# Feed-forward products with 512 moving columns, later start loads, and token parts of x made beside the router logits

## The reference

```python
def _hier_moe(x, w_grp, b_grp, w_exp, b_exp, w_gate, w_up, w_down):
    grp_logits = (xf @ w_grp + b_grp)                # 4 groups
    exp_logits = (xf @ w_exp + b_exp)                # 32 experts, 8 in a group
    # best group, two best experts in it, then for each chosen expert e:
    hdn = jax.nn.silu(xb @ w_gate[e]) * (xb @ w_up[e])
    y = hdn @ w_down[e]                              # weighted and added per token
# second block, four times, d_ff = 2816:
    y = (silu(x @ gate) * (x @ up)) @ down           # x <- norm(ALPHA * x + 0.5 * y)
```

## Time and profile before

| | us |
|---|---|
| median of 3 runs | 2418.55 |
| the 3 runs | 2409.77, 2421.46, 2418.55 |
| the profiled execution | 2419.57 |
| its span, first to last instruction | 2417.6 |
| PE busy | 2214.3 |
| DVE busy | 1076.5 |
| ACT busy | 734.3 |

### The profile page before, as it was taken

The page is one execution under the profiler, slowest core; times in us unless marked ns, Lnnn a source line. Parts: engine busy times, 40 slices in busy tenths (PEclk is TensorE's granted clock), DMA queues, the critical chain, the costliest instruction groups (busy, mean ns, idle before and its releaser), DMA issues.

```text
span 2417.6 us, 32311 instructions
## 1 busy us (share of the span) xinstructions
PE 2214.3 (92%) x13534; PEld 1641.1 (68%) x13534; DVE 1076.5 (45%) x1606; ACT 734.3 (30%) x1123; POOL 60.4 (2%) x62
## 2 busy tenths in 40 slices
PE   7978998799898889978988999988999999888998
PEld 7874443343377845424433899888998999788997
DVE  4663221121167722211212655666556555666555
ACT  3432110011134321101111444443444444543443
POOL 0010000000010100000000000001000000001000
PEclk9989999899997799999999999989999999979999
DMA  9437999999962389999999746523554565423551
GB/s 295 132 141 313 420 421 421 417 420 420 400 205 69 133 328 420 421 420 416 420 421 401 242 165 209 161 84 114 183 192 163 186 209 192 140 70 116 181 192 52
DMA packets 231548, 622.79 MB, mean 258 GB/s; under 512 B 15456, under 2 KB 166944, under 8 KB 182112
## 3 DMA queue, kind: packets, MB, share of 16 engines
q1 hardware_dynamic: 225952, 604.99, 66.1%
q0 software_dynamic: 3040, 10.78, 1.3%
q10 hardware_dynamic: 2400, 4.83, 0.6%
HBM read 619.51 MB, written 1.05 MB: 257 GB/s over the span
## 4 chain that ended last, share of the span: by engine, by line
PE 42%; DMA 6%; DVE 4%; ACT 1%; issue 1%; SPq 0%; POOL 0%; DVEq 0%; ACTq 0%
PE bank L228 28%; PE bank L1486 9%; PE bank L1326 3%; DMA wide_tables<-in_moe_w_up 1%; DMA x_tok<-in_moe_w_up 1%; DMA ring<-in_moe_w_up 1%; DMA w_parts<-in_moe_w_up 1%; DMA ring<-in_ffn_gate 1%; PE bank L1647 1%; DVE w_low L429 1%; DVE x_tok L674 0%; DVE x_tok L663 0%; DVE bn L652 0%; PE bank L469 0%; ACT w_high L422 0%
## 5 line engine op out<-in xcount | busy, mean ns | idle before, releaser
L429 DVE TENSOR_TENSOR w_low<-ring,w_high 128x1024 fp32r<-128x1024 f32 x364 | 440.6, 1225 | 374.2 <-ACT w_high L422 374.1
L228 PE MATMUL bank<-xT_high,w_high 128*128 128x256 f32 x1712 | 488.3, 285 | 20.4 <-DVE xT_low L491 12.0
L228 PE MATMUL bank<-xT_low,w_high 128*128 128x256 f32 x1712 | 486.5, 284 | 0.0
L228 PE MATMUL bank<-xT_high,w_low 128*128 128x256 f32 x1712 | 486.2, 284 | 0.0
L422 ACT ACTIVATE w_high<-ring 128x1024 fp32r<-128x1024 f32 x364 | 376.6, 1052 | 296.2 <-PE bank L228 274.6
L1326 PE MATMUL bank<-ring,arena 128*64 128x512 f32 x1344 | 339.4, 594 | 18.2 <-DMA ring<-in_moe_w_up 6.0
L228 PEld LDWEIGHTS bank<-xT_high,w_high 128*128 128x128 f32 x1712 | 330.2, 193 | 26.1 <-DVE xT_low L491 12.0
L228 PEld LDWEIGHTS bank<-xT_low,w_high 128*128 128x128 f32 x1712 | 330.4, 193 | 2.8
L228 PEld LDWEIGHTS bank<-xT_high,w_low 128*128 128x128 f32 x1712 | 330.3, 193 | 0.0
L1326 PE MATMUL bank<-w_parts,arena 128*64 128x512 f32 x768 | 259.1, 596 | 14.4 <-DMA w_parts<-in_moe_w_up 6.6
L1326 PEld LDWEIGHTS bank<-ring,arena 128*64 128x64 f32 x1344 | 111.2, 137 | 230.5 <-issue 221.6
(11 more groups left out here) (285 smaller groups left out, 2860.4 us busy)
## 6 DMA issues: line engine op xcount, KB each, us to landing
ring<-in_moe_w_gate SPq DMA_DIRECT2D x56, 1024.0 KB, 23.6
ring<-in_moe_w_up SPq DMA_DIRECT2D x56, 1024.0 KB, 22.7
ring<-in_moe_w_down SPq DMA_DIRECT2D x56, 1024.0 KB, 26.1
ring<-in_ffn_gate SPq DMA_DIRECT2D x44, 1024.0 KB, 5.7
ring<-in_ffn_up SPq DMA_DIRECT2D x44, 1024.0 KB, 5.4
ring<-in_ffn_down SPq DMA_DIRECT2D x44, 1024.0 KB, 5.3
w_parts<-in_moe_w_down SPq DMA_DIRECT2D x32, 1024.0 KB, 26.6
w_parts<-in_moe_w_gate SPq DMA_DIRECT2D x32, 1024.0 KB, 22.1
```

The lines of the kernel that those rows point to most:

```text
L228: ins = e.matmul(out, lhs, rhs, start=first and i == 0, stop=last and i == len(parts) - 1)
L429: e.tensor_tensor(lo, src, hi.bitcast(F32), ALU.subtract).then_inc(*S.low.tell(key))
```

## The change

Four edits:

1. In the feed-forwards, gate and up get a PSUM bank each. For a K tile one matmul of 512 moving columns takes `xh` and `xl` together (they now lie in one tensor, `x_parts`) by the high weights, and one of 256 adds high x by low weights. The halves of the bank are added afterwards: ACT copies the first half to SBUF, DVE adds the second half; then silu, now from SBUF, and the product.
2. The token parts get places of their own: `x_tok_high` in the wide tables, `x_tok_low` in `mixT`. ACT makes each block right after the transposed parts of that block, and DVE makes the low parts before it waits for the logits. The two places are no longer lent to the ring; instead the tiles of `xh` and `xl` are lent, once the router's products are done.
3. The first norm's rows are loaded once the seventh weight tile has landed.
4. The load of the `dif` tables goes from ACT's queue to SP's, behind the first weight tile.

```diff
-LENT = ("wide", "mix", 1, 2, 3, "arena", "arena", 0, "x_tok")
+LENT = (1, 2, 3, "arena", "arena", 0, "x_high", "x_low", "x_tok")
...
             e.activation(k.xh[at], view, ACT.Copy).then_inc(*S.x_high.tell((n, tb, half)))
+        if layer is not None:
+            token_part_act(e, k, n, layer, tb)
...
+    token_parts_dve(e, k, layer)
     e.wait_ge(*S.used["router", layer])
...
-    token_parts_dve(e, k, layer)
...
-            mm(e, bank[:, half * T:(half + 1) * T], three([((hi[:, j, :], lo[:, j, :]), (k.xh[:, j, :], k.xl[:, j, :])) for j in range(KT)])
-               ).then_inc(*S.used.tell(key))
+            for j in range(KT):
+                e.matmul(pairs(bank[:, :]), hi[:, j, :], k.x_parts[:, :, j, :], start=j == 0, stop=False)
+                ins = e.matmul(bank[:, 0:T], lo[:, j, :], k.xh[:, j, :], start=False, stop=j == KT - 1)
+            ins.then_inc(*S.used.tell(key))
...
+            e.wait_ge(*S.used["ffn", i, name, f])
+            if f >= 2:
+                e.wait_ge(*S.ffn_low[i, f - 2])
+            e.activation(out[:, f % 2, :], k.banks["ffn", i, name + " sum", f][:, 0:T], ACT.Copy).then_inc(*S.ffn_first.tell((i, name, f)))
+        e.wait_ge(*S.dve_out["ffn", i, "gate sum", f])
+        e.activation(k.ffn_gate[:, f % 2, :], k.ffn_gate[:, f % 2, :], ACT.Silu).then_inc(*S.ffn_silu.tell((i, f)))
...
+            e.wait_ge(*S.ffn_first[i, name, f])
+            e.tensor_tensor(out[:, f % 2, :], out[:, f % 2, :], bank[:, T:2 * T], ALU.add).then_inc(*S.dve_out.tell(("ffn", i, name + " sum", f)))
...
-        loads_sp(e, k, 0, FIRST_LOADS)
+        loads_sp(e, k, 0, 1)
+        e.dma_start(k.tables[:, start:middle], A["tables"][:, start:middle]).then_inc(*S.tables_loaded["dif"].land("dif"))
+        loads_sp(e, k, 1, FIRST_LOADS)
...
-        e.dma_start(k.tables[:, first:middle], A["tables"][:, first:middle]).then_inc(*S.tables_loaded["dif"].land("dif"))
...
+        e.wait_ge(*S.tables_loaded["ident"]["ident"])
+        e.wait_ge(*k.ring.landed(ev(EV_ORDER[FIRST_LOADS - 1])))
         load_norm_pool(e, k, 0)
-        e.wait_ge(*S.tables_loaded["ident"]["ident"])
```

More of the change, by code:

```diff
@@ L475, in x_parts_at, with split_x_act @@
     return view, (slice(0, P), slice(4 * half, 4 * half + 4), block(tb))
-def split_x_act(e, k, n):
+def split_x_act(e, k, n, layer=None):
     S = k.S
@@ L1225, in expert_tiles, with token_part_act @@
     return b
-def token_parts_act(e, k, layer):
+def token_part_act(e, k, n, layer, tb):
     S = k.S
-    e.wait_ge(*S.used["router", layer])
-    for tb in range(NB):
-        e.activation(k.x_tok_high[:, tb, :, :], by_kk(k.x_tok[:, tb, :]), ACT.Copy).then_inc(*S.token_high.tell((layer, tb)))
+    e.wait_ge(*S.x_tok[n, tb, 1])
+    e.wait_ge(*S.low["router", layer])
+    e.activation(k.x_tok_high[:, tb, :, :], by_kk(k.x_tok[:, tb, :]), ACT.Copy).then_inc(*S.token_high.tell((layer, tb)))
 def by_kk(v):
@@ L1489, in ffn_pe @@
     for f in range(FT):
-        bank = k.banks.open(e, B_BANKS, ("ffn", i, "hidden", f))
-        for half, name in enumerate(("gate", "up")):
+        for name in ("gate", "up"):
             key = ("ffn", i, name, f)
+            bank = k.banks.open(e, B_BANKS, ("ffn", i, name + " sum", f))
             _, hi, lo = split_views(k, key)
             e.wait_ge(*S.low[key])
-            if f == 0 and half == 0:
+            if f == 0 and name == "gate":
                 x_ready(e, k, n, 1)
-            mm(e, bank[:, half * T:(half + 1) * T], three([((hi[:, j, :], lo[:, j, :]), (k.xh[:, j, :], k.xl[:, j, :])) for j in range(KT)])
-               ).then_inc(*S.used.tell(key))
+            for j in range(KT):
+                e.matmul(pairs(bank[:, :]), hi[:, j, :], k.x_parts[:, :, j, :], start=j == 0, stop=False)
+                ins = e.matmul(bank[:, 0:T], lo[:, j, :], k.xh[:, j, :], start=False, stop=j == KT - 1)
+            ins.then_inc(*S.used.tell(key))
         if f >= FFN_LAG:
@@ L1517, in ffn_act @@
     for f in range(FT):
-        for _ in range(2):
+        for name, out in (("gate", k.ffn_gate), ("up", k.ffn_hidden)):
             ffn_fill(e, k, i, n, n + 1, split_act)
             n += 1
-        bank = k.banks["ffn", i, "hidden", f]
-        e.wait_ge(*S.used["ffn", i, "up", f])
-        if f >= 2:
-            e.wait_ge(*S.ffn_low[i, f - 2])
-        e.activation(k.ffn_silu[:, f % 2, :], bank[:, 0:T], ACT.Silu).then_inc(*S.ffn_silu.tell((i, f)))
+            e.wait_ge(*S.used["ffn", i, name, f])
[4 more added lines that the diff above has]
+        e.activation(k.ffn_gate[:, f % 2, :], k.ffn_gate[:, f % 2, :], ACT.Silu).then_inc(*S.ffn_silu.tell((i, f)))
         e.wait_ge(*S.dve_out["ffn", i, "hidden", f])
@@ L1540, in ffn_dve @@
     for f in range(FT):
-        for _ in range(2):
+        for name, out in (("gate", k.ffn_gate), ("up", k.ffn_hidden)):
             ffn_fill(e, k, i, n, n + 1, split_dve)
             n += 1
-        bank = k.banks["ffn", i, "hidden", f]
+            bank = k.banks["ffn", i, name + " sum", f]
+            e.wait_ge(*S.ffn_first[i, name, f])
+            e.tensor_tensor(out[:, f % 2, :], out[:, f % 2, :], bank[:, T:2 * T], ALU.add).then_inc(*S.dve_out.tell(("ffn", i, name + " sum", f)))
         e.wait_ge(*S.ffn_silu[i, f])
-        e.tensor_tensor(k.ffn_hidden[:, f % 2, :], k.ffn_silu[:, f % 2, :], bank[:, T:2 * T], ALU.mult).then_inc(*S.dve_out.tell(("ffn", i, "hidden", f)))
+        e.wait_ge(*S.dve_out["ffn", i, "up sum", f])
+        e.tensor_tensor(k.ffn_hidden[:, f % 2, :], k.ffn_gate[:, f % 2, :], k.ffn_hidden[:, f % 2, :], ALU.mult
+                        ).then_inc(*S.dve_out.tell(("ffn", i, "hidden", f)))
         e.wait_ge(*S.ffn_high[i, f])
@@ L2377, in lent @@
     S, what = k.S, LENT[extra]
-    if what == "wide":
-        return [(S.product, ("gate_log", 1)) if run else (S.dve_step, ("decay", 3))]
-    if what == "mix":
-        return [(S.low, ("router", run))]
+    if what in ("x_high", "x_low"):
+        return [(S.used, ("router", run))]
     if what == "arena":
@@ L2573, in sp_program @@
     if part == 0:
-        middle, second = k.cols["ret_cos"][0], k.cols["ones"][0]
+        start, middle, second = (k.cols[name][0] for name in ("dif_cos", "ret_cos", "ones"))
         for b in range(NB):
             e.dma_start(k.x_tok[:, b, :], A["x"][0, block(b), :]).then_inc(*S.x_loaded[b].land(0))
-        loads_sp(e, k, 0, FIRST_LOADS)
+        loads_sp(e, k, 0, 1)
+        e.dma_start(k.tables[:, start:middle], A["tables"][:, start:middle]).then_inc(*S.tables_loaded["dif"].land("dif"))
+        loads_sp(e, k, 1, FIRST_LOADS)
         e.dma_start(k.tables[:, middle:second], A["tables"][:, middle:second]).then_inc(*S.tables_loaded["ret"].land("ret"))
@@ L2626, in act_program @@
         ev_act(e, k)
-        split_x_act(e, k, 0)
-        token_parts_act(e, k, 0)
+        split_x_act(e, k, 0, 0)
         scaled_x_act(e, k, 0, 0)
```

20 lines of the change are left out of this document (11 added, 9 removed).

## The result

The changed kernel takes 2391.24 us (median of 4 runs, 2385.30 to 2400.20); the kernel before took 2420.01 in the same series (4 runs, 2409.77 to 2422.62). The ratio is 0.9892, 95 % interval 0.9844 to 0.994. The forecast was 2394.5 with a range of 2384 to 2408. The profiled execution of the changed kernel is the slowest of its four, 2400.20, with a span of 2398.3 us.

What follows compares the result with a forecast made beforehand. Loads bound the experts' stages, PE alone the feed-forwards; mixers are PE, ACT and DVE chains. Savings of 15.2 + 5.4 + 3.5 = 24.1 us from 2419.6 give 2395.5 profiled, 2394.5 as median, range 2384 to 2408.

Steps and rivals of the forecast that it cites:

- Feed-forward products: Gate and up matmuls on PE: one fixed part less per K tile saves 15.2 us, between 11.5 and 18.8.
- The page's rule: Feed-forward matmuls: rival with a fixed part of 2.5 ns, saving only 3.5 us there; 2407 us, chance 0.03.
- Added steps at cost 0: Feed-forward tiles: the added ACT copies and DVE sums fit beside PE's stream and cost 0.
- Token parts: Router to gather, both layers: less PE idle time and a faster clock save 5.4 us, between 4.0 and 8.5.
- Lending at cost 0: Expert weight stream: replacement slots, 4 MB issued at about 190 us, load before the first refill; cost 0.
- Start: First weight tile: norm rows and dif load behind it, so work starts earlier; 3.5 us, between 1.1 and 5.0.
- Early gains don't arrive: Rival: clock falls elsewhere, later lent slots delay the stream, feed-forward term at its low end; 2406 us, chance 0.08.

Runs made afterwards that it cites:

- ffn_only: Kernel before with edit 1 alone (gate and up by 512 and 256 columns, sums on ACT and DVE): 2403.18 us against 2415.28, ratio 0.9958.
- grouped_again: Second run of the changed kernel with each gate or up tile's eight 512-column matmuls first, then the eight of 256: 2382.98 us, ratio 0.9855 to the kernel before.
- double_steps: Changed kernel with the added ACT copies and DVE sums made twice, second results unused: 2388.16 us, ratio 0.9881 to the kernel before.
- low_late: Changed kernel with DVE's low token parts put back behind the choice of experts: 2392.71 us, ratio 0.9905 to the kernel before.
- Tokens_only: Kernel before with edit 2 alone (token parts in own places, made beside the logits; other slots lent): 2411.49 us, ratio 0.9984.
- grouped: Changed kernel with each gate or up tile's eight 512-column matmuls first, then the eight of 256: 2381.99 us, ratio 0.9852 to the kernel before.
- again: The changed kernel run once more, unaltered: 2390.02 us against 2418.95 for the kernel before, ratio 0.9881.
- adjacent: Changed kernel with high and low x of a K tile side by side, 512 columns in one run: 2392.96 us, ratio 0.9905 to the kernel before.

## Why the prediction was right

The forecast won, and its sum of 24.1 us has 23.1 +- 1.9 opposite at equal clock: 15.5, 3.3 and 4.3 for the parts, where it had 15.2, 5.4 and 3.5. That the sum fits so closely is in part luck: the second part was 2 us too large, and by this measure the others gave 0.3 and 0.8 more than forecast. The medians of the two series give 28.8 and 28.9. In the second series the changed kernel's mean clock was 0.003 above before's, which is 5 us by the line; in the first the kernel before's clock is on record for the profiled execution alone, so its surplus stays open. The low and the high end of the forecast were added up as 2387 to 2402 against the profiled execution; 2419.6 - 16.6 is 2403. Step by step:

- **Feed-forward products, 15.2 us.** Measured 12.9 us by the stages of the changed kernel and 14.1 in ffn_only (15.5 +- 1.6 at equal clock): inside 11.5 to 18.8, below the value taken. The term is 1 to 2 us too large because the 512-column distance was put at the middle, 0.2292, between two cases; it is 0.233, a little above the upper one. My reason for going below it was the one distance from 512 to 256 columns. The trace before has 68 of these, and they take 0.2267 us, the lower bound; yet in a stream that alternates at every step the distance is 0.233. So a single change does not foretell a stream of changes. The shorter distance of the 256-column matmul, 0.117 instead of 0.120, gave part of it back. Each feed-forward became 2.9 to 3.5 us shorter, not 3.8.
- **The page's rule.** The rival by which only 3.5 us would come has fallen: 13 to 14 us came. For a feed-forward stream of this kind the fixed part is 0.230 - 0.213 = 17 ns at 512 columns and 0.119 - 0.107 = 12 ns at 256 (grouped_again). The Trainium skill, page "TensorE: Matmul & The Clock Gate", section "Back-to-back issue gap", has 2.5 ns for both, for a gap in isolation; these traces don't agree.
- **Added steps at cost 0.** Right, with a margin that double_steps shows.
- **Token parts, 5.4 us.** The mechanism was right: idle time 1.39 (1.4 predicted), and low_late puts all of it on DVE's order. Two sizes were off and cancelled in part. I had the late copy of the logits cost 0.6 us in layer 1 alone and called it hidden in layer 0 by 0.9. It costs 0.6 to 0.7 us in both (PE waits 1.24 to 1.32 where it waited 0.60 to 0.67), except where the router's products ran at the lower clock. The 4.86 us of idle time in the earlier trace rows on which I had relied came from router products that ran at the lower clock in that execution; they took 0.21 us each there and 0.12 in most others. And the clock in the gather gave 1.7 to 2.5 us a layer, not 0.7: in 15 of 16 passages with an idle time of 1.4 us it stayed up. Without the clock the term is 2 x (2.33 - 0.65) = 3.4 us. Tokens_only has 3.3 +- 1.3 at equal clock; that fits, but that the line takes out just the gather's clock is not shown.
- **Lending at cost 0.** Right: the experts of layer 1 last 452.2 to 452.8 us in every kernel, the first refill follows 3.7 us behind the first expert product, and the shift passes through to the end of the stage.
- **Start, 3.5 us.** Right in size: 4.3 +- 1.3 at equal clock, 3.1 of the 4.0 us at the first product by the norm's rows. Wrong in one sentence: "From there to 208 the mixer has no wait for loads, so it passes on." No wait for loads came, but the clock can take it all back in the mixer. The term had the clock's swing at the start alone (1.3 up, 1.8 down); at 67 us it is about 4, as large as the gain itself. The prediction had a few us for the clock in the mixers in its range, but not in this term.
- **Early gains don't arrive** was given 0.08. In the profiled execution of the changed kernel this is what happened in the even mixer, and the stage gained nothing there; the medians contain it to a degree that I can't separate.

The best version of all is grouped, 2382 to 2383 us in two series: one loop in place of one.

Not settled: why eight matmuls of a length together are faster, why grouped's mean clock is higher, and whether a shifted start makes the low stretch at 67 us more frequent. A single profile per kernel can't tell; it would take many profiled executions of the same kernel.

## What to carry to other kernels

In a stream that PE bounds, fewer and longer matmuls save part of what each one costs beyond its columns: 10 to 12 ns for every two of 256 columns made into one of 512 here. The order of the matmuls is worth trying too: eight of a length together were 2 ns a K tile faster than taking turns. When an in-order engine has work that isn't urgent between two urgent steps, move it to where that engine idles, but look at which step then waits for it in an execution at full clock. Divide what a change does into what it does at equal clock and what it does by the clock; a gain of 4 us in a mixer was invisible in the profile of the changed kernel and whole in that of double_steps.

## What the runs showed of the hardware

- Matmuls of 512 and 256 columns in turn take 0.233 and 0.117 us (after), in groups of eight 0.229 and 0.119 (grouped, grouped_again): about 2 ns for a pair. The cause is open; the single distances at the changes of length speak against the change as such.
- A moving operand in two pieces 8 KB apart is as fast as one run: 0.3501 and 0.3498 us for a K tile (after, again) against 0.3497 (adjacent).
- Behind 3.7 us of idle time (and the same small products before it) PE began the gather at the lower level of the clock in 10 of 10 passages; behind 1.4 us it stayed at the upper level in 15 of 16.
- Executions of one kernel on one core differ by 10 to 19 us in 2400, and mean granted clock accounts for most of it: 1.8 us per 0.001, with 1.8 us of scatter left. A single stretch of 10.2 us at the lower level (1.2 GHz), which comes or stays away with the same code, is worth about 4 us of it.
